# Attention's half of the mixed output product placed among the S5 products, the S5 skip term inside its convolution kernel, and the residual read back by token halves

## The reference, cut to what matters

```
u, q, k, v = split(rms_norm(x) @ w_mix_in)           # 512 columns each
a = dilated_attention(q, k, v)                       # 512 wide, 8 heads
y = S5(u) + d_skip * u                               # 32 groups of 16 channels, diagonal state space
y = gelu(y);  s = y * sigmoid(y @ w_glu + b_glu)     # 512 wide
x = x + rms_norm(concat(a, s) @ w_mix_out) * post_g  # 1024 -> 1024
```

## Time and profile before

| | us |
|---|---|
| median of 3 runs | 3405.72 (3404.87 to 3407.22) |
| the profiled execution | 3401.22 |
| its span in the profile | 3399.6 |
| TensorE busy in the span | 3215.0 (95%) |
| VectorE, ScalarE, GpSimd busy | 2066.8, 1293.3, 376.1 |
| the dilated attention | about 2310 to 2466 |
| S5 with its GLU | 2466 to 2573 |
| output product, token half 0, half 1 | 2573 to 2620, 2620 to 2664 |

### The profile page before, as it was taken

The page is one execution under the profiler, slowest core; times in us unless marked ns, Lnnn a source line. Parts: engine busy times, 40 slices in busy tenths (PEclk is TensorE's granted clock), DMA queues, the critical chain, the costliest instruction groups (busy, mean ns, idle before and its releaser), DMA issues.

```text
span 3399.6 us, 39667 instructions
## 1 busy us (share of the span) xinstructions
PE 3215.0 (95%) x15804; PEld 2529.8 (74%) x15804; DVE 2066.8 (61%) x2774; ACT 1293.3 (38%) x1907; POOL 376.1 (11%) x405
## 2 busy tenths in 40 slices
PE   8998899999999998899999999998879899999998
PEld 6765576878777786578888877785567778888877
DVE  5545566664555646777776556675564777766334
ACT  2564434442525344643233224313434443223123
POOL 1000000110302011100000003140011300000012
PEclk9999999999999999899999999999989999999999
DMA  6210111222423122332224243322153332224232
GB/s 155 49 41 5 54 50 52 72 87 75 100 50 106 50 88 74 101 110 82 80 76 164 95 143 102 110 64 84 17 107 130 108 121 87 75 99 166 80 113 99
DMA packets 363254, 299.39 MB, mean 88 GB/s; under 512 B 55104, under 2 KB 324896, under 8 KB 362784
## 3 DMA queue, kind: packets, MB, share of 16 engines
q1 hardware_dynamic: 340800, 215.17, 22.0%
q0 software_dynamic: 22272, 81.69, 7.3%
HBM read 240.32 MB, written 52.95 MB: 86 GB/s over the span
## 4 chain that ended last, share of the span: by engine, by line
PE 74%; DVE 12%; ACT 6%; DMA 5%; issue 3%; SPq 1%; POOL 0%; ACTq 0%; DVEq 0%; POOLq 0%
PE PS L364 41%; PE PS L2450 12%; PE PA L2450 7%; DMA CDX<-ssd_decays 3%; PE PS L864 2%; PE PA L875 1%; DVE WL L328 1%; DVE CDX L1999 1%; PE PB L1778 1%; DVE XL L2127 1%; PE PB L887 1%; ACT PP L975 1%; DMA WS<-in_ffn_w_out_dram 1%; PE PA L404 1%; PE PB L1781 1%
## 5 line engine op out<-in xcount | busy, mean ns | idle before, releaser
L364 PE MATMUL PS<-XH,WH 128*128 128x512 f32 x1744 | 603.6, 405 | 37.9 <-DVE XL L2127 20.2
L364 PE MATMUL PS<-XL,WH 128*128 128x512 f32 x1744 | 580.3, 392 | 0.0
L364 PE MATMUL PS<-XH,WL 128*128 128x512 f32 x1744 | 579.4, 391 | 0.0
L321 ACT ACTIVATE WH<-WS 128x1024 fp32r<-128x1024 f32 (+1 forms) x243 | 240.3, 992 | 843.4 <-PE PS L364 793.0
L364 PEld LDWEIGHTS PS<-XH,WH 128*128 128x128 f32 x1744 | 326.5, 189 | 137.0 <-DVE XL L2127 27.9
L364 PEld LDWEIGHTS PS<-XH,WL 128*128 128x128 f32 x1744 | 329.2, 189 | 70.3
L364 PEld LDWEIGHTS PS<-XL,WH 128*128 128x128 f32 x1744 | 329.1, 189 | 69.4 <-issue 2.0
L328 DVE TENSOR_TENSOR WL<-WS,WH 128x1024 fp32r<-128x1024 f32 (+1 forms) x243 | 284.8, 1172 | 142.8 <-ACT WH L321 142.5
L364 PE MATMUL PS<-TQH,WH 128*128 128x512 f32 x448 | 161.5, 395 | 7.0 <-DVE WL L328 7.0
L364 PE MATMUL PS<-TQL,WH 128*128 128x512 f32 x448 | 160.2, 392 | 0.0
L364 PE MATMUL PS<-TQH,WL 128*128 128x512 f32 x448 | 160.1, 392 | 0.0
(11 more groups left out here) (683 smaller groups left out, 6167.2 us busy)
## 6 DMA issues: line engine op xcount, KB each, us to landing
RAW<-in_ffn_w_in_dram SPq DMA_DIRECT2D x36, 1024.0 KB, 5.3
WS<-in_ffn_w_out_dram SPq DMA_DIRECT2D x48, 512.0 KB, 3.5
WS<-in_ssd_w_in_dram SPq DMA_DIRECT2D x40, 512.0 KB, 3.7
DEC<-ssd_decay_sums SPq DMA_DIRECT2D x32, 512.0 KB, 4.1
WS<-in_ffn_w_in_dram SPq DMA_DIRECT2D x32, 512.0 KB, 3.8
CDX<-ssd_decays SPq DMA_DIRECT2D x56, 256.0 KB, 4.8
TQF<-ffn_hidden POOLq DMA_DIRECT2D x14, 1024.0 KB, 8.3
x_residual<-ACC POOLq DMA_DIRECT2D x6, 2048.0 KB, 8.0
```

Source lines behind the costliest of these rows:

```text
L321: nc.scalar.activation(WH[:, s, 0:cols], WS[:, s, 0:cols], ACT.Copy).then_inc(W_HI[s], 1)
L364: last = nc.tensor.matmul(PS[s][0:width, c], w[:, s, k * width:(k + 1) * width], x[:, k, c], start=(k == 0 and j == 0), stop=(k == kt - 1 ...
```

## The change

The output product's attention half for token half 0 becomes eight blocks of its own (`att_block(m)`: 4 k x 3 products of 512 columns, 256 KB of weights), placed among the S5 products; ACT copies each result into PARTS[m]. In the tail the blocks of h = 0 hold only the S5 half, with 256 KB each, and DVE's eviction adds PARTS[m]. The tail's h = 1 is as before, with its inputs in other places. The attention's high parts (XHA) and remainders (XLA) are made beside the attention steps: XHA after step 5 of the next head pair, XLA after step 6. The states' inputs and the kernel of half 1 now use PA and PB, after those of half 0 have been read out, since PS belongs to the new blocks. The skip term is no longer added on DVE: SKIPS holds a 16 x 16 diagonal for each group, and one more small product adds it to the kernel's lag 0; the order of the products in it changes. The 82 products of `keep_busy` are gone. The GLU blocks 0 and 1 do their first three k before the last y part is ready. Parts of DVE's and ACT's order move, several tiles lie elsewhere, and the rates RE and RI are loaded later. The residual is read back in four transfers of 1024 KB: half 0 once the S5 remainders are made, half 1 after the sixth block of the tail.

```diff
+ATT_FIRST = 7
...
+def att_block(m):
+    return B_ATT + m + (4 if m >= ATT_FIRST else 0)
...
+        for part in range(3):
+            att_products(pe, 0, range(part, part + 1))
             dil.norm_tensor(pe, 3, part)
+    def att_products(pe, m, ks=range(4)):
+        block_products(pe, att_block(m), XHA, XLA, kt=4, ks=ks, h=0, after=(lambda k: pe.wait_ge(ATT_LO, XLD_END + k + 1)) if m == 0 else None)
...
+    def att_high(act, p):
...
+        nc.scalar.activation(XHA[:, p], ACC[:, p], ACT.Copy).then_inc(ATT_HI, 1)
...
+    def att_low(dve, p):
...
+        nc.vector.tensor_tensor(XLA[:, p, c], ACC[:, p, c], XHA[:, p, c].bitcast(F32), ALU.subtract).then_inc(ATT_LO, 1)
...
     def s5_scalar(act, st):
...
+        def keep_att(m):
+            b = att_block(m)
+            act.wait_ge(BLOCK_DONE[b % 2], times(b))
+            if m == 1:
+                act.wait_ge(S5_PRODUCTS, S5STATE[1])
+            nc.scalar.activation(PARTS[m][:], PS[b % 2][:, half(0)], ACT.Copy).then_inc(PS_READ[b % 2], 1)
...
     def s5_tensor(pe):
...
+        s5_states(pe, 0)
+        att_products(pe, 1)
+        att_products(pe, 2)
+        s5_kernel(pe, 0)
+        pe.wait_ge(S5_COPIES, S5KC + 2)
+        s5_states(pe, 1)
+        att_products(pe, 3)
+        att_products(pe, 4)
+        s5_kernel(pe, 1)
+        att_products(pe, 5)
+        s5_y(pe, 0)
+        s5_y(pe, 1)
+        s5_y(pe, 2)
+        att_products(pe, 6)
+        s5_y(pe, 3)
+        glu_products(pe, 0, range(3))
+        glu_products(pe, 1, range(3))
+        glu_products(pe, 0, range(3, 4))
+        glu_products(pe, 1, range(3, 4))
+        glu_products(pe, 2)
+        glu_products(pe, 3)
+        for m in range(ATT_FIRST, KT):
+            att_products(pe, m)
+        for m in range(KT):
+            block_products(pe, tail_block(2, 0, m), XH[:, 0:4], XH[:, 4:8], kt=4, h=0,
+                           after=(lambda k: pe.wait_ge(MIXLO, XLD_END + k + 1)) if m == 0 else None)
...
+    def s5_kernel(pe, h):
...
+        for t in range(8):
+            for r in range(2):
+                rows, g = slice(64 * r, 64 * r + 64), 16 * h + 2 * t + r
+                out = PAB[r][0:16, t * P:(t + 1) * P]
+                for ri in range(2):
+                    nc.tensor.matmul(out, BBK[rows, ri, 8 * h + t], CA[rows, ri, 8 * h + t, 0:S5_T].rearrange("p k c -> p (k c)"),
+                                     start=(ri == 0), stop=False)
+                last = nc.tensor.matmul(out[:, 0:S5_CH], IDENT[0:S5_CH, 0:S5_CH], SKIPS[:, g], start=False, stop=True)
-            stt(S5Y[:, k], MU[:, k], vec("dsk", k), S5Y[:, k], ALU.mult, ALU.add).then_inc(S5_RESULTS, 1)
...
     def s5_vector(dve, st):
...
+        rotate(0)
+        scan(0)
+        lo(att_block(3))
+        lo(att_block(4))
+        rotate(1)
+        scan(1)
+        lo(att_block(5))
+        scan(2)
+        lo(att_block(6))
+        scan(3)
...
     def reload_pool(pool, u, b_last):
-        parts = [(RL_X[:], XRES)] if u != 2 else [(RL_A[:], XRES[0:4]), (RL_B[:], XRES[4:8])]
+        pool.wait_ge(MIXLO, XLD_END + 4)
+        for h in range(2):
+            if h == 1:
+                b = B_MIXOUT + 5
+                pool.wait_ge(BLOCK_DONE[b % 2], times(b))
+            for dst, src in ((RL_A, XRES[0:4]), (RL_B, XRES[4:8])):
+                pool.dma_start(dst[:, :, half(h)], src[:, :, half(h)].rearrange("k p t -> p k t")).then_inc(RESID if h == 0 else S5TOE, 16)
```

More of the change, by code:

```diff
@@ L3227, in s5_vector, with gated @@
+        dve.wait_ge(S5_PRODUCTS, S5Yp + 8)
+        lo(B_GLU)
+        z_low(0)
+        z_low(1)
+        lo(B_GLU + 1)
+        z_low(2)
+        for p in range(4):
+            att_low_late(dve, p)
+        z_low(3)
+        def gated(m):
             b = B_GLU + m
             dve.wait_ge(PS_READ[b % 2], times(b))
-            tt(ACC[:, 4 + m], ZF[:, m], T[m % 2][:], ALU.mult).then_inc(S5_RESULTS, 1)
-            split_lo(dve, b + 2, cols=cols_of(b + 2))
-        dve.wait_ge(S5_RESULTS, S5GLU + 4)
@@ L3265, in s5_scalar @@
         gelu(1)
+        hi(B_GLU + 1)
+        keep_att(6)
         copy_y(3)
@@ L3268, in s5_scalar, with gate @@
         gelu(3)
-        for m in range(4):
+        def gate(m):
             b = B_GLU + m
@@ L3291, in s5_tensor @@
             last.then_inc(S5_PRODUCTS, 1)
+            if k == 1:
+                att_products(pe, 0, range(3, 4))
         pe.wait_ge(UGL, 16 * S5_T)
         pe.wait_ge(S5_COPIES, S5GIN + 4)
-        pairs = ((PA, PB), (PS[0], PS[1]))
-        for h, pair in enumerate(pairs):
-            for t in range(8):
-                q = 8 * h + t
-                for ri in range(2):
-                    for r in range(2):
-                        rows = slice(64 * r, 64 * r + 64)
-                        last = nc.tensor.matmul(pair[ri][rows, t * P:(t + 1) * P], GIN[:, q, ri, rows], UG[:, 2 * q + r], start=True, stop=True)
-            last.then_inc(S5_PRODUCTS, 1)
@@ L3303, in s5_tensor @@
-        pe.wait_ge(S5LD, 80)
-        for h, pair in enumerate(pairs):
-            pe.wait_ge(S5ROT, h + 1)
-            for t in range(8):
-                for ri in range(2):
-                    for r in range(2):
-                        rows = slice(64 * r, 64 * r + 64)
-                        last = nc.tensor.matmul(pair[r][0:16, t * P:(t + 1) * P], BBK[rows, ri, 8 * h + t],
-                                                CA[rows, ri, 8 * h + t, 0:S5_T].rearrange("p k c -> p (k c)"),
-                                                start=(ri == 0), stop=(ri == 1))
-                        if t == 7 and ri == 1:
-                            last.then_inc(S5_PRODUCTS, 1)
@@ L3315, in s5_tensor @@
-        for k in range(4):
-            h, pair = k // 2, pairs[k // 2]
-            if k % 2 == 0:
-                pe.wait_ge(S5_COPIES, S5KC + 2 * h + 2)
-                if k == 0:
-                    keep_busy(PA, 11)
-                pe.wait_ge((UD, S5TOE)[h], (16, 0)[h] + 16 * S5_T)
-            pe.wait_ge(S5_RESULTS, S5V + k + 1)
-            for t in range(4):
-                q, c = 4 * k + t, slice((4 * (k % 2) + t) * P, (4 * (k % 2) + t + 1) * P)
-                y = [pair[r][:, c] for r in range(2)]
-                for r in range(2):
-                    nc.tensor.matmul(y[r], TOE[:, 2 * q + r], UG[:, 2 * q + r], start=True, stop=False)
-                for ri, s in enumerate((VR, VI)):
-                    for r in range(2):
-                        rows = slice(64 * r, 64 * r + 64)
-                        last = nc.tensor.matmul(y[r], CA[rows, ri, q, 1:].rearrange("p k c -> p (k c)"), s[rows, q],
-                                                start=False, stop=(ri == 1))
-                        if t == 3 and ri == 1:
-                            last.then_inc(S5_PRODUCTS, 1)
@@ new lines, in glu_products, with s5_states @@
+    def glu_products(pe, m, ks=range(4)):
+        block_products(pe, B_GLU + m, ZH, ZL, kt=4, ks=ks, after=(lambda k: pe.wait_ge(ZLO, XLD_END + k + 1)) if m < 2 else None)
+    def s5_states(pe, h):
+        for t in range(8):
+            q = 8 * h + t
+            for ri in range(2):
+                for r in range(2):
+                    rows = slice(64 * r, 64 * r + 64)
+                    last = nc.tensor.matmul(PAB[ri][rows, t * P:(t + 1) * P], GIN[:, q, ri, rows], UG[:, 2 * q + r], start=True, stop=True)
+        last.then_inc(S5_PRODUCTS, 1)
@@ new lines, in s5_y @@
+    def s5_y(pe, k):
+        if k == 0:
+            pe.wait_ge(S5_COPIES, S5KC + 4)
+            pe.wait_ge(UD, 16 + 16 * S5_T)
+        if k == 2:
+            pe.wait_ge(S5TOE, 16 * S5_T)
+        if k >= 2:
+            pe.wait_ge(S5_COPIES, S5YC + 2 * k - 2)
+        pe.wait_ge(S5_RESULTS, k + 1)
+        for t in range(4):
+            q, c = 4 * k + t, slice((4 * (k % 2) + t) * P, (4 * (k % 2) + t + 1) * P)
+            y = [PAB[r][:, c] for r in range(2)]
+            for r in range(2):
+                nc.tensor.matmul(y[r], TOE[:, 2 * q + r], UG[:, 2 * q + r], start=True, stop=False)
+            for ri, s in enumerate((VR, VI)):
+                for r in range(2):
+                    rows = slice(64 * r, 64 * r + 64)
+                    last = nc.tensor.matmul(y[r], CA[rows, ri, q, 1:].rearrange("p k c -> p (k c)"), s[rows, q],
+                                            start=False, stop=(ri == 1))
+                    if t == 3 and ri == 1:
+                        last.then_inc(S5_PRODUCTS, 1)
```

294 lines of the change are left out of this document (196 added, 98 removed).

## The result

The changed kernel takes 3419.77 us (median of 7 runs, 3414.15 to 3423.70), the kernel before 3404.77 us (7 runs, 3401.81 to 3407.22), measured beside it. The ratio is 1.0044, with a 95% interval of 1.0034 to 1.0053: **15 us slower**, where 3400 us and a gain were forecast. The profiled execution of after took 3416.07 us, its span 3414.4, the mean granted clock 0.978.

What follows compares the result with a forecast made beforehand. TensorE, busy 95%, was taken as the bound, with a chain through DVE, ACT and transfers in S5. 21.5 us gained in the tail less 15.9 lost before it gave 5.6, so 3405.7 became 3400; range 3382 to 3410.

Steps and rivals of the forecast that it cites:

- Attention at next to nothing: Attention's high parts and block 0 quarters would fit into existing waits; cost taken as 0, four missed copies would be 4 us.
- the 21.8 us of products leaving token half 0: In the tail, 96 products of 0.227 us leave half 0 and enter S5; a block costs 2.72 us instead of 5.44.
- The contention of the residual's load: In the tail, the residual's load competes with weight loads for the DMA; 5 us, bounds 0 and 10.
- The stretch from y over to GLU over: From the start of y part 3's last product to the GLU's end, through store, reload, GELU and remainder; 33.7 us.
- The step with the largest error: the tail: After the GLU, half 0 would end after 25.2 us plus 5 of contention, instead of 51.7; 21.5 us gained.
- that of part 3 behind GELU 1, at 2553.3: ACT's copy of y part 3 would follow GELU 1, at 2553.3 us, with part 3 ending at 2550.6.
- The kernel products: S5 convolution kernel: 0.77 us a group from sequential passes, narrow product and two shape changes; 12.3 us a half.
- The rival of the half clock: Kernel products run at half clock, 6.9 us more a half, 13.8 in all, 3414 us; chance 0.12.
- What runs in the same rows cannot run together: Reason given for kernel products in the new order running in sequence: one group costs four passes, 0.43 us.
- the bound of 9.0 us: Kernel half with products in sequence and no price for shape changes: 9.0 us.
- The claim that the narrow product makes this edit dear: In the kernel products, shape changes around the skip product drain the engine; without it 9.0 us a half would hold.
- the late tail: Rival: the tail does not keep up, weight loads behind both residual bursts; 5 us more, 3405 us; chance 0.06.

Runs made afterwards that it cites:

- the seventh kernel: The fourth's kernel with the residual's halves issued later: half 0 after the last sum of half 0, half 1 after the fourth sum of half 1; 3383.51 us.
- the first kernel: The changed kernel with GpSimd issuing the residual's second half after its sum of the sixth tail block, not waiting ahead of all sums (also experiment 1); 3412.39 us.
- the fourth's: The changed kernel with three edits: residual's second half later, GLU weights ahead of y's stores, four big kernel products alternating with narrow ones behind; 3387.76 us.
- experiment 2: The changed kernel with the weight loads of GLU blocks 0 and 1 issued ahead of all stores of y; 3415.88 us.
- experiment 5: The changed kernel without the narrow skip products, order of the others kept, so the result lacks the skip term; 3404.24 us, one run.
- experiment 3: The changed kernel with the four big products alternating between row groups as before and both narrow products behind them; 3406.03 us.
- the ninth kernel: The seventh kernel with attention block 5 moved behind y part 0 and block 6 behind y part 3; 3384.16 us.
- twelfth kernels: The seventh kernel measured again, unchanged; 3384.73 us.
- The tenth kernel: The ninth kernel without the narrow products, so the result lacks the skip term; 3380.99 us.
- experiment 11: The ninth kernel with kernel steps t and t + 4 joined: eight big products, then four narrow ones; 3386.01 us.
- experiments 8: The fourth's kernel without the narrow products, so the result lacks the skip term; 3388.57 us.
- the sixth kernel: The kernel before with both products of one row group ahead of the other's, no narrow product; 3407.30 us, one run.

## Why the prediction was wrong

It forecast a gain of 5.6 us and the trace shows a loss of 16.1. The 22 us between them fall in three stretches: 6.6 up to the end of y (0.3 us behind the row "y over", which is the start of the last product), 6.6 from there to the end of the GLU, 8.8 in the tail.

**Right.** Attention at next to nothing, as far as the traces can tell; kernel 0 starting 10.2 us after the states; the states of half 1 just behind the copies; the 21.8 us of products leaving token half 0, which the seventh kernel shows at 2.72 us a block with a tail of 31.1 us (25.2 + 5.44 = 30.6 by the working). The contention of the residual's load, forecast at 5 us, measured 2.4 us between the first kernel's tail and the seventh's and 4.4 between the fourth's and the seventh's. The stretch from y over to GLU over, forecast at 33.7, takes 33.5 once the weights' order is put right (experiment 2).

**The step with the largest error: the tail.** The prediction put 5 us of contention on the load of the residual and nothing on its place in GpSimd's queue. The working counted the load's bytes, but not that the wait of its second half for block 5 stands ahead of five sums of squares, that ACT needs those sums, and that the next weights' split is behind ACT's squares. The tail is 8.8 us longer than forecast; undoing that wait alone gave 10.9 us in the trace and 7 in the median (experiment 1). The 10.9 exceed the 8.8 because the contention itself was forecast too high. The wait is new: before, the whole residual is issued in one go, ahead of all sums, and GpSimd's queue holds no wait for TensorE among them.

**The step "that of part 3 behind GELU 1, at 2553.3".** The copy of part 3 came 10.1 us after y was over, not 2.7. Between GELU 1 and this copy stands `hi(B_GLU + 1)`, which waits for a load that SyncE issues only behind the stores of part 2. The working named these stores and the GELU, and left out the weights between them. That order too is new: before, the loads of the first two GLU blocks stand ahead of all stores of y. The stretch to the end of the GLU is 6.6 us longer than forecast; experiment 2 gave back 7.1 in that stretch and 4 in the median.

**The kernel products.** Their term was 12.3 us a half, built of passes in sequence (0.43), the narrow product (0.13) and two changes (0.2). Measured at full clock is 0.68 a group instead of 0.77 (10.9 us a half), a narrow product 0.055 and a change 0.09. The halves still took 15.4 and 14.2 us from their first product to the end of the last, because 4.5 and 3.3 us of half clock came on top; another 2.0 us came in rotation 1, which started late behind states at half clock (attention blocks 3 and 4 end at the same moment as its product SI, at 2510.1). The rival of the half clock, given 0.12, was thus right in its mechanism and too large in its price (13.8 us against 7.8). That its time of 3414 is the nearest to the measured one is luck: the half clock made 7.8 us, and the tail and the weights, which it did not hold, 15.4. And one sentence was wrong in its reason: "What runs in the same rows cannot run together" doesn't apply to two groups in different rows, whatever their order. Without the narrow product the bound of 9.0 us was in truth 3.5 (experiment 5). The claim that the narrow product makes this edit dear holds: its place between the groups cost 14 us, nearly the whole loss of the change (experiment 3). Of that, two halves at 5.0 us are the lost overlap at full clock, and the half clock, 7.8 us in after and in no half of the third kernel, comes on top. These 17.8 us are 15.6 in the sum of the trace; kernel 0 alone started 1.4 us later in the third.

**The range.** It held no term for an engine standing at the wrong place of its queue: the late tail had 5 us and 0.06, and no term stood for a wait of ACT at the GLU's weights. Both waits could be read in the order of the changed code, and both only make it slower.

**What stays open.** Why the clock fell in after's kernel 0 at 2485.5, with TensorE busy since 2481.38, in its kernel 1 at 2515.8, busy since 2504.57, and in the ninth kernel's y part 0, was not tried by itself (no kernel put full-size products in between). In the third, fourth, seventh, ninth and twelfth kernels, whose halves last 5.9 to 6.0 us, it did not fall within one. What it is in the narrow product that ends the overlap is known in part: a further product of the same shape between the groups does no harm (the fifth kernel has PA's second one there), but its shape, its rows (0 to 15 for both groups) and its column count were changed together. The tenth kernel's gain of 3.2 us can't be told from none.

## What to carry to other kernels

When a change moves or shortens a stage, write out each engine's queue around it in program order, DMA queues too, and ask of every wait in it what stands behind. Here a load of weights put behind stores, and a wait for a block's end put ahead of sums that others need, cost 7 and 11 us in the trace, each more than the whole gain that was forecast. Place products of another tile shape behind the groups that can overlap, not between them: that alone was worth 14 us of 3420. Longer runs of them save 0.09 us for each change of shape, too little to show in the time here (experiment 11). Don't count a shortened wait as a gain before it is known what is late next: twice here (experiments 8 and 9) another queue or the clock took back what was saved. And don't count from a zero without asking what lies ahead of it.

## What the runs showed of the hardware

- Products of two row groups start 0.01 us apart even when the program puts one group wholly behind the other (experiment 5). With a narrow product of 16 rows between the groups they follow each other: 1.36 us for two groups instead of 0.44 (after and experiment 5), and 0.73 with both narrow products behind them (experiment 3).
- A change of the tile's shape costs 0.09 us and a narrow product of two passes 0.055 (experiments 3, 5 and 11). By the rule in the Trainium skill, "TensorEngine Tiling (Array Packing)", Key Properties, a change of mode drains the engine; the trace agrees with the 0.09 us.
- The busy time of the page and the granted clock are two things: after's window 2490:2500 has 8.90 us busy of 10 at a clock of 0.50, window 2500:2510 of the third kernel 9.15 us at 1.00.
- The start of the states varies by up to 9 us from trace to trace, and the wait for UG from 1.3 to 6.4 us; between before and the sixth kernel, which are alike ahead of it, by 4.6 us.
- Behind a wait of 3.48 us or more (nine traces) the products of the states start at half clock, 0.43 us a group, behind 2.61 us or less (five traces) at full clock, 0.22.
